# Sums and differences of weight pieces computed by GpSimd instead of VectorE, in a three-block transformer forward pass

## The reference

```
h = rms_norm(x, norm)
x = x + scale * ((silu(h @ w_gate) * (h @ w_up)) @ w_down)      # w_gate, w_up: 1024 x 2816, w_down: 2816 x 1024
```

## Time and profile before

| what | value |
|---|---|
| median of 3 runs | 3310.09 us (3305.27 to 3312.91) |
| the profiled execution | 3311.36 us, of which the span is 3309.2 us |
| PE busy | 3181.7 us, 96% of the span |
| DVE busy | 2182.7 us, 66% |
| ACT busy | 1490.5 us, 45% |
| POOL busy | 75.7 us, 2% |
| DMA | 304.01 MB, 92 GB/s on average |
| granted TensorE clock | 0.986 of full speed |

### The profile page before, as it was taken

How to read it: one execution, slowest core, us unless ns; L and a number is a source line. 1 busy time by engine, 2 the same in 40 slices (tenths; PEclk the granted TensorE clock), 3 DMA queues, 4 the chain that set the end, 5 groups by cost and what they waited for, 6 DMA issues and landing times.

```text
span 3309.2 us, 37762 instructions
## 1 busy us (share of the span) xinstructions
PE 3181.7 (96%) x15170; PEld 2601.1 (79%) x15170; DVE 2182.7 (66%) x3452; ACT 1490.5 (45%) x2314; POOL 75.7 (2%) x153
## 2 busy tenths in 40 slices
PE   9999988999999999999989899999999999899998
PEld 7888766677887888788967677888889777787887
DVE  7685776745457656856787664456676666768656
ACT  5453445544345435534444554334353445445333
POOL 0000010100000000000010100000000100000000
PEclk9999999999999999999999999999999999999999
DMA  4331331322333234233232222241331544133231
GB/s 178 103 96 59 101 91 46 96 90 77 96 127 115 75 94 131 68 95 108 71 99 72 67 82 83 89 159 58 102 115 54 106 86 61 58 122 114 68 102 60
DMA packets 234335, 304.01 MB, mean 92 GB/s; under 512 B 11696, under 2 KB 180016, under 8 KB 234160
## 3 DMA queue, kind: packets, MB, share of 16 engines
q1 hardware_dynamic: 227408, 284.73, 29.2%
q0 software_dynamic: 6608, 16.79, 1.7%
q10 hardware_dynamic: 144, 0.10, 0.0%
HBM read 293.17 MB, written 2.10 MB: 89 GB/s over the span
## 4 chain that ended last, share of the span: by engine, by line
PE 70%; DVE 20%; ACT 7%; issue 3%; DMA 1%; POOL 0%; SPq 0%; DVEq 0%; ACTq 0%
PE bank L592 21%; PE bank L604 13%; PE bank L597 13%; PE bank L606 8%; PE bank L599 8%; DVE k_wl L824 4%; ACT k_wh L806 3%; DVE k_xraw L812 2%; PE bank L1403 2%; PE bank L1051 1%; PE bank L1452 1%; PE bank L1436 1%; DVE k_sc L1138 1%; DVE k_xwl L824 1%; DVE k_sc L841 1%
## 5 line engine op out<-in xcount | busy, mean ns | idle before, releaser
L824 DVE TENSOR_TENSOR k_wl<-k_raw,k_wh 128x1024 fp32r<-128x1024 f32 (+1 forms) x314 | 368.9, 1175 | 377.0 <-ACT k_wh L806 375.5
L806 ACT ACTIVATE k_wh<-k_raw 128x1024 fp32r<-128x1024 f32 (+1 forms) x314 | 319.8, 1019 | 442.3 <-PE bank L604 302.3
L824 DVE TENSOR_TENSOR k_wl<-k_xraw,k_wh 128x1024 fp32r<-128x1024 f32 (+1 forms) x279 | 318.3, 1141 | 212.3 <-ACT k_wh L806 211.2
L806 ACT ACTIVATE k_wh<-k_xraw 128x1024 fp32r<-128x1024 f32 (+1 forms) x279 | 276.7, 992 | 369.1 <-PE bank L604 190.6
L592 PE MATMUL bank<-k_xh,k_wh 128*128 128x512 f32 x840 | 364.6, 434 | 0.0
L604 PE MATMUL bank<-k_xh,k_wl 128*128 128x512 f32 x840 | 334.4, 398 | 4.7 <-DVE k_cv L1831 3.2
L597 PE MATMUL bank<-k_xl,k_wh 128*128 128x512 f32 x840 | 333.7, 397 | 0.0
L592 PE MATMUL bank<-k_h,k_wh 128*128 128x512 f32 x696 | 272.2, 391 | 0.0
L604 PE MATMUL bank<-k_h,k_wl 128*128 128x512 f32 x696 | 271.2, 390 | 0.0
L597 PE MATMUL bank<-k_h,k_wh 128*128 128x512 f32 x696 | 271.0, 389 | 0.0
L592 PE MATMUL bank<-k_wh,k_S 128*128 128x512 f32 (+1 forms) x656 | 246.3, 376 | 0.0
(11 more groups left out here) (377 smaller groups left out, 6658.9 us busy)
## 6 DMA issues: line engine op xcount, KB each, us to landing
k_raw<-in_w_in SPq DMA_DIRECT2D x153, 512.0 KB, 3.7
k_xraw<-in_ffn_w_gate SPq DMA_DIRECT2D x51, 512.0 KB, 4.2
k_xraw<-in_ffn_w_down SPq DMA_DIRECT2D x47, 512.0 KB, 4.5
k_xraw<-in_ffn_w_up SPq DMA_DIRECT2D x45, 512.0 KB, 4.6
k_raw<-in_w_out SPq DMA_DIRECT2D x28, 512.0 KB, 3.3
k_xraw<-in_ffn_w_gate SPq DMA_DIRECT2D x26, 384.0 KB, 3.2
k_raw<-in_ffn_w_down SPq DMA_DIRECT2D x26, 384.0 KB, 3.0
k_raw<-in_ffn_w_up SPq DMA_DIRECT2D x19, 512.0 KB, 4.6
```

What stands on the lines that cost most here:

```text
L806: e.activation(self.pair[c.pair][0][:, 0:n], self.unit[c.src][:, 0:n], ACT.Copy).then_inc(*self.act.up(("wh", c.i)))
L824: e.tensor_tensor(lo[:, 0:n], self.unit[c.src][:, 0:n], hi[:, 0:n].bitcast(F32), ALU.subtract).then_inc(*self.dve.up(*marks))
```

## The change

The 200 mix operations go from VectorE's program into a program of GpSimd, with a semaphore of their own for its steps. VectorE keeps the subtractions that split the chunks. A split that reads a mix's result now waits for GpSimd's step, a mix that comes after a split waits for VectorE's, each mix waits for the one before it on GpSimd, and buffers that a mix reads last are given back by GpSimd's step. The new line 828 is the mix, line 821 the split on VectorE; all lines behind it are 12 higher than in the kernel before.

```diff
-        self.ready[out] = ("dve", ("mix", out))
+        self.ready[out] = ("pool", ("mix", out))
...
-            self.units.append((self.home.pop(name), ("dve", ("split", i))))
+            self.units.append((self.home.pop(name), ("pool" if post else "dve", ("split", i))))
...
+    def dve_weights(self, e):
+        for c in self.p.chunks:
+            n = c.kt * c.n
+            yield c.split + 0.5
+            hi, lo = self.pair[c.pair]
+            e.wait_ge(*self.act.sig(("wh", c.i)))
+            marks = [("wl", c.i)] + [("split", c.i)] * (not c.post)
+            e.tensor_tensor(lo[:, 0:n], self.unit[c.src][:, 0:n], hi[:, 0:n].bitcast(F32), ALU.subtract).then_inc(*self.dve.up(*marks))
+
     def mix(self, e, x, n, marks):
         out, a, b, op, waits, key = x
         for ref in waits:
             e.wait_ge(*self.sig(ref))
-        e.tensor_tensor(self.unit[out][:, 0:n], self.unit[a][:, 0:n], self.unit[b][:, 0:n], op).then_inc(*self.dve.up(key, *marks))
-
-    def dve_weights(self, e):
+        e.wait_ge(*self.pool_.here())
+        e.tensor_tensor(self.unit[out][:, 0:n], self.unit[a][:, 0:n], self.unit[b][:, 0:n], op).then_inc(*self.pool_.up(key, *marks))
+
+    def pool_weights(self, e):
+
         for c in self.p.chunks:
             n = c.kt * c.n
             for x in c.pre:
                 yield c.split - 2.0
                 self.mix(e, x, n, ())
-            yield c.split + 0.5
-            hi, lo = self.pair[c.pair]
-            e.wait_ge(*self.act.sig(("wh", c.i)))
-            marks = [("wl", c.i)] + [("split", c.i)] * (not c.post)
-            e.tensor_tensor(lo[:, 0:n], self.unit[c.src][:, 0:n], hi[:, 0:n].bitcast(F32), ALU.subtract).then_inc(*self.dve.up(*marks))
             for j, x in enumerate(c.post):
                 yield c.split + 0.6
                 e.wait_ge(*self.dve.sig(("wl", c.i)))
...
-        s = [self.pool_start(e)]
+        s = [self.pool_start(e), self.pool_weights(e)]
```

More of the change, by code:

```diff
@@ L126, in __init__ @@
         self.activation, self.preload_act_table_set = engine.activation, engine.preload_act_table_set
+class PoolLane(Lane):
+    def __init__(self, engine):
+        super().__init__(engine)
+        self.tensor_tensor = engine.tensor_tensor
 class VectorLane(Lane):
@@ L410, in __init__ @@
         self.bank = [nc.alloc_psum_tensor(f"bank{i}", [P, T], F32)[:, :] for i in range(8)]
-        self.pe, self.act, self.dve = (Steps(nc, f"s_{n}_steps") for n in ("tensor", "scalar", "vector"))
-        self.steps = {"pe": self.pe, "act": self.act, "dve": self.dve}
+        self.pe, self.act, self.dve, self.pool_ = (Steps(nc, f"s_{n}_steps") for n in ("tensor", "scalar", "vector", "pool"))
+        self.steps = {"pe": self.pe, "act": self.act, "dve": self.dve, "pool": self.pool_}
         for i in range(RAW + XRAW):
@@ L2520, in _ @@
         def _(e):
-            k.pool(Lane(e))
+            k.pool(PoolLane(e))
         @block.scalar
```

## The result

The changed kernel takes 3324.26 us (median of 5 runs, 3320.57 to 3327.05), the kernel before 3309.98 us beside it (5 runs, 3305.27 to 3312.91). The ratio is 1.0044 with a 95% interval from 1.0029 to 1.0059: 14.3 us slower. The forecast was 3326 us, slower. The number was right. Its place in the kernel was not, as the waits show.

A forecast was written before the change was run, and what follows sets the result against it. The prediction took TensorE, busy for 96% of the span, as the bound. To the profiled 3311.4 us it added 15 us at the block ends and nothing elsewhere, giving 3326 us, with a range of 8 in 10 from 3297 to 3376.

The forecast's parts named there:

- The two engines take turns: In SBUF, VectorE operations with two inputs there wait for a running GpSimd mix to end, up to 2.1 us.
- The 222 us that leave VectorE: Over five feed-forward parts, moving 200 mixes takes 222 us of work off VectorE, almost none on TensorE's path.
- A wide mix at 2.1 us: On GpSimd, a mix of 1024 columns takes 2.1 us, twice ScalarE's time to read one such input.
- The split in front of this chain comes later too: Before the block-end chain, splits wait about 1 us per mix met, so the chain ends 0.25 to 1.25 us later.
- The term of +15 us: At block ends, before TensorE's transposes: 20 places, each 0.75 us later, add 15 us.
- a wash: Rival at block ends: VectorE has caught up, so the earlier split cancels the mix's delay; 3311 us, chance 0.20.
- I put the matmuls' waits for rests at 0 to 5 us, and take 0: In the block stretches, TensorE's waits for the remainder of a split chunk add 0 to 5 us, counted as 0.
- Saturation: Rival in the blocks: VectorE needs 30.4 us per 28 us stretch, adding 60 us; 3371 us, chance 0.22.
- the lead of the splits: In the blocks, splits finish ahead of their matmuls, by 3.6 us at the tight place, covering a 2.4 us delay.
- No turns: Rival: both engines run side by side, so the 14.3 us wait at the transposes goes; 3297 us, chance 0.18.
- The load buffers and GpSimd's DMAs: Load buffers return about 1 us later and the mixers' DMAs share no stretch with mixes; both add nothing.

The follow-up runs named there:

- the run with fills: Changed kernel with each of the 200 GpSimd mixes replaced by three constant fills of its output, which read nothing; sums left out; 3284.31 us in one run.
- the run with only the 20 mixes on GpSimd: Kernel before, with only four mixes of the first block in each feed-forward part moved to GpSimd, the other 180 on VectorE; 3326.37 us, ratio 1.0054.
- the run with the held T3: Changed kernel with 20 first-block mixes back on VectorE, and later blocks' first-half T3 mix held until the previous block's line 1150 ends; 3324.20 us, ratio 1.0047.

## Why the prediction was right in its number and wrong in its place

- **The two engines take turns: right.** Line 1150 was blocked (2.40 us), splits last up to 3.46 us, and fills that read nothing block nobody. In the Trainium skill, SBUF — State Buffer, "Who interferes with whom", the rule names just these two sides, VectorE with two inputs in SBUF and GpSimd reading SBUF, and not a GpSimd instruction that only writes; the mixes and the fills agree with it.
- **The 222 us that leave VectorE: a sum of durations.** Of its busy time they are 200 us (1982.6 in the run with fills), since successive instructions overlap. Nothing in the forecast hangs on it.
- **A wide mix at 2.1 us: too low,** it is 2.40 us, and 1.84 us at 768 columns. The ratio to VectorE's 1.22 us is 1.97. The Trainium skill has 1.96 in GPSIMD Engine Reference, "Performance versus the Vector engine", and the trace agrees with it better than with my reading of ScalarE's rows.
- **"The split in front of this chain comes later too": the step that failed.** The sum was 20 places at 0.75 us, of which 0.25 came from the block end itself and the rest from that split. The first piece was fair: it is 0.4 us. The second had the wrong sign: the split comes 0.6 us earlier. VectorE, rid of the mixes ahead of it, had caught up by then, though single splits were blocked for longer than the 1 us taken (one of block 1 lasts 3.37 us, at 101.80). The term of +15 us came out as 11.9 - 14.3 = -2.4 us. This is the rival "a wash" in its mechanism, at the place for which it was written.
- **"I put the matmuls' waits for rests at 0 to 5 us, and take 0": wrong in its place, and its pair was not looked for.** The waits for rests at the starts came to 4.2 us, within the 0 to 5 us, but not where the prediction looked. The larger term, the wait for line 1081 with what TensorE's clock loses behind it, was not in the sum at all, though its row stood in the earlier trace rows with one wait for each part. I read the busy stretches of the blocks and not the start of a part, where VectorE and ScalarE work in a chain with no lead. The change costs 18.3 us there.
- **Saturation: did not come.** In the blocks VectorE is busy for 23.15 of 28 us, with the blocking in it, and the lead of the splits holds. Its mark, waits for line 821, appeared, but in 7 places, six at the starts and one before the first mix.
- **No turns: excluded.** The run with fills shows about what it would have been worth: 3284 us, where the prediction had 3297; the wait for line 1081 goes as well.
- The load buffers and GpSimd's DMAs cost nothing that the waits show, as taken.

So two errors cancelled, by luck: for the blocks the forecast had +15 us where the runs show -4.2, for the starts of the parts 0 where they show +18.3.

**Open.** When the clock falls behind such a wait is not known. In the profiled execution of the changed kernel it fell in parts two to five and not in the first. In the run with only the 20 mixes on GpSimd the wait was 2.3 us in all five parts, and it fell in the second alone, though that kernel's median is no lower. The kernel before has one long wait there, 2.68 us in the first part, and the clock fell behind it. So the 1.6 us are no fixed part of the cost, and how they spread over other executions was not measured. The run with fills frees the block ends and the starts at once, and it is one run; what each was worth there was not separated.

## What to carry to other kernels

An elementwise operation with two inputs in SBUF that goes from VectorE to GpSimd frees VectorE of little (of 200 us of busy time moved here 197 came back as blocking), so it should go, if at all, where VectorE does nothing that another engine waits for step by step: look for such chains at the seams between stages, and not only where VectorE is fullest. In this kernel the blocking of those chains came to 28 us of the 197, and the whole loss lay at the parts' starts, where they stand. See first whether the operation can stand behind the chain on its own engine; that alone brought 12.7 us. To find where a change costs, run it for the suspected part alone and for all but that part, and see whether the two add up to the whole within their spread.

## What the runs showed of the hardware that was not expected

- The blocking goes both ways. A mix that starts just behind a split takes 3.2 to 3.45 us in place of 2.40 us, as in the run with the held T3 (3.26 us, begun 0.2 us after a split of 1.22 us).
- Short instructions are hit hardest: two operations of some 0.38 us each (line 971) took 3.66 us, with one mix running when the first began and the next from 1339.54 to 1341.93 us, the end of the pair being at 1342.21.
- Fills of GpSimd, 0.95 us for 1024 columns and three in a row, leave VectorE's two-input operations at their 0.75 and 1.22 us.
- A wait of TensorE of 2.3 us was followed by eight matmuls at the level of 1.2 GHz (granted clock 0.58 in the 4 us around them), which cost 1.6 us more, two thirds of the wait itself. It happened in four of five like places of the changed kernel, and in one of five where only the 20 mixes were on GpSimd.
